# A decoder layer on eight cores: finer dependency records, loads in order of need, seven block products in half of the down projection, norm gains applied at the transposes, and the causal mask as a minimum

## The reference, cut to what matters

```python
n = rms_norm(h, tm_pre_g)                        # sub-layer 1
u, v, q, k, v_att, g_a, g_b = jnp.split(n @ w_in, IN_SPLITS, axis=-1)
u = jax.nn.gelu(u); v = layer_norm(jax.nn.gelu(v), ln_v_g, ln_v_b)
y_a = chunked_spatial_gating(u, v, w_spatial, b_spatial) @ w_branch_a
y_b = moba_attention(partial_rope(q), partial_rope(k), v_att) @ w_branch_b   # causal inside a block
y = (sigmoid(g_a) * y_a + sigmoid(g_b) * y_b) @ w_tm_out
h = h + rms_norm(y, tm_post_g)
...
h = h + rms_norm(cross_attention(rms_norm(h, ca_pre_g), rms_norm(mem, mem_norm_g), ...), ca_post_g)
n = rms_norm(h, ffn_pre_g)
y = (silu(n @ w_gate) * (n @ w_up)) @ w_down     # hidden width 5632
h = h + rms_norm(y, ffn_post_g)
```

## Time and profile before

| | |
|---|---|
| three runs | 3659.61, 4012.02 and 4272.59 us |
| median of the three | 4012.02 us |
| profiled execution, slowest core (core 3) | span 3663.7 us |
| spans of the eight cores | 3637.2 to 3663.7 us |
| mean granted TensorE clock, die 0 and die 1 | 0.983 and 0.984 of full speed |
| PE busy | 3425.0 us, 93% |
| DVE, ACT busy | 46%, 33% |

### The profile page before, as it was taken

How to read it: one execution, slowest core, us unless ns; L and a number is a source line. 1 busy time by engine, 2 the same in 40 slices (tenths; PEclk the granted TensorE clock), 3 DMA queues, 4 the chain that set the end, 5 groups by cost and what they waited for, 6 DMA issues and landing times.

```text
span 3663.7 us, 52891 instructions; the slowest of 8 cores (3637.2 to 3663.7 us)
## 1 busy us (share of the span) xinstructions
PE 3425.0 (93%) x17866; PEld 1641.4 (45%) x17866; DVE 1691.9 (46%) x3470; ACT 1201.3 (33%) x2157; POOL 226.8 (6%) x306
## 2 busy tenths in 40 slices
PE   5989999999888899999887999999999988999997
PEld 3534444444355544545543444444444433444443
DVE  3764465222267746444776555555555620001222
ACT  4633323334477600445652222222222220000110
POOL 1100000000000000000110000000000010000000
PEclk9999999999999999999999999999999999999999
DMA  9225566666742354545665545554454556346564
GB/s 195 74 37 92 96 108 116 110 105 105 136 99 76 82 145 133 152 149 172 172 178 87 94 85 98 87 88 83 83 98 81 93 187 221 105 141 231 210 220 157
DMA packets 339097, 455.97 MB, mean 124 GB/s; under 512 B 29456, under 2 KB 288784, under 8 KB 317712
## 3 DMA queue, kind: packets, MB, share of 16 engines
q0 software_dynamic: 192048, 157.30, 28.4%
q1 hardware_dynamic: 146784, 295.29, 25.0%
HBM read 475.60 MB, written 148.90 MB: 170 GB/s over the span
## 4 chain that ended last, share of the span: by engine, by line
PE 77%; DVE 9%; DMA 6%; issue 4%; ACT 3%; DVEq 0%; POOL 0%; ACTq 0%; SPq 0%; POOLq 0%
PE ps L316 76%; DVE acc L342 2%; DVE fw0r L336 1%; DMA wv<-w_in 1%; PE ps L319 1%; DVE fw2r L336 1%; DMA ht<-HIDT 1%; ACT ffs L329 1%; DMA fw0r<-w_fg 1%; DMA fr0r<-w_fg 1%; DMA HIDT<-ffo 1%; DMA memx<-mem 1%; DVE fpf L332 0%; DVEq L262 0%; DMA gto<-gains 0%
## 5 line engine op out<-in xcount | busy, mean ns | idle before, releaser
L316 PE MATMUL ps<-wd,ht 128*128 128x512 f16 x2816 | 614.4, 381 | 30.5 <-DMA ht<-HIDT 29.7
L316 PEld LDWEIGHTS ps<-wd,ht 128*128 128x128 f16 x2816 | 276.3, 98 | 368.5 <-issue 40.7
L349 ACT COPY fpf<-ps 128x512 f32<-128x512 f32 x336 | 196.1, 584 | 504.6 <-PE ps L316 504.6
L316 PE MATMUL ps<-n1op,ws1r 128*128 128x512 f16 x1024 | 235.7, 383 | 11.0 <-ACT pf L349 11.0
L316 PE MATMUL ps<-n1op,ws0r 128*128 128x512 f16 x1024 | 234.1, 381 | 3.8 <-ACT pf L349 3.8
L349 ACT COPY pf<-ps 128x512 f32<-128x512 f32 x256 | 149.6, 586 | 268.6 <-PE ps L316 267.4
L316 PE MATMUL ps<-RBH,ma 128*128 128x512 f16 x1024 | 226.2, 379 | 0.0
L332 DVE TENSOR_TENSOR fpf<-ps,fpf 128x512 f32<-128x512 f32 x168 | 115.6, 688 | 195.9 <-PE ps L316 158.3
L316 PE MATMUL ps<-n1op,ws0t 128*128 128x512 f16 x768 | 178.1, 382 | 11.0 <-DVE n1op L332 7.5
L329 ACT ACTIVATE junk<-ps 128x512 bf16<-128x512 f32 x128 | 76.1, 595 | 333.8 <-PE ps L316 331.3
L329 ACT ACTIVATE pT<-ps 128x512 bf16<-128x512 f32 (+1 forms) x320 | 160.5, 531 | 69.6 <-PE ps L316 67.1
(11 more groups left out here) (226 smaller groups left out, 4831.1 us busy)
## 6 DMA issues: line engine op xcount, KB each, us to landing
ht<-HIDT SPq DMA_DIRECT2D x40, 1408.0 KB, 7.8
H<-yr SPq DMA_DIRECT2D x32, 1024.0 KB, 9.1
HIDT<-ffo SPq DMA_DIRECT2D x88, 256.0 KB, 8.8
WDH<-w_fd POOLq DMA_DIRECT2D x44, 512.0 KB, 14.3
ws0r<-w_in POOLq DMA_DIRECT2D x16, 1024.0 KB, 13.2
ws1r<-w_in POOLq DMA_DIRECT2D x16, 1024.0 KB, 13.4
GS<-stgh SPq DMA_DIRECT2D x64, 256.0 KB, 4.6
xr<-x SPq DMA_DIRECT2D x16, 1024.0 KB, 6.7
```

Source lines behind the costliest of these rows:

```text
L316: self.S.add("pe", lambda e: e.matmul(out, lhsT, rhs, start=start, stop=stop, **kw), reads, writes)
L349: self.S.add("act", lambda e: e.copy(out, in_), reads, writes)
```

## The change

- **Records.** Tiles that one engine writes in pieces get a record for each piece (`parts=4` for the attention accumulators, `yr`, `cob`, `cqt`), so a piece waits for its own piece. Some DMA semaphores are marked `exact`: a wait is for that DMA and not for the newest on the semaphore. Waits of one instruction on one semaphore are merged.
- **Loads.** x tiles 2 to 5 and the constants wait for parts of `wv`; `wv` comes in eight DMAs; x uses four buffers; the `w_sp` transposes come later. The memory tokens are normed and transposed during blocks 20 to 30 and kept in HBM (`MTD`), their weights are converted to f16 in HBM (`WKH`) during blocks 2 to 17. The first head is loaded ahead of these weights, and `gto` beside `wo`.
- **First blocks.** Two gate blocks come first; the first two products of both quads are done before the third of either. The sum S1 and the slots' sums are in the plan. The same interleaving starts the FFN.
- **Mask.** `dm` is 0 above the diagonal and 3e38 elsewhere; DVE takes the minimum with the exponentials instead of the second matmul.
- **Norm gain of the FFN.** `fgain` is gone; the copy after the transposes multiplies by the gain (`f_c2`).
- **Down projection.** Columns 0 to 1023 go by seven block products, with blocks of 22x128 hidden by 128 tokens and 22x128 hidden by 256 columns. The weights are kept in a layout of their own (`WD7`).
- **End.** The last 512 columns are done in two halves, and the last tile's four output parts have a record and a semaphore each.
- Durations and latencies in the plan are new numbers; the DVE statistics of the layer norm have two instructions fewer.

```diff
-            if so.sem is p.dsem:
+            if so.sem is p.dsem and not so.exact:
...
     blocks = []
+    for i in range(2):
+        blocks.append(("g", i, 5120 + i * 256))
...
+            gate = {2: [bwv[kc][0] for kc in range(8)], 4: [bwv[kc][1] for kc in range(8)], 6: env[("x", 4)][1] if tt == 6 else []}
+            B.dma("sp", ap, x[tt * 128:(tt + 1) * 128, :], d, gate.get(tt, []), bufs)
...
-            if diag:
-                B.mm(ps_[:, 0:128], identb[:], dm[:], False, True, [bcon2], [psb_])
...
+        if diag:
+            def f_cm(pk=pk):
+                p_, pb_ = env[pk]
+                B.tt(p_[:, 0:128], p_[:, 0:128], dm[:], ALU.min, [pb_, bcon3], [pb_])
+            ex = T("dve", 0.1, f_cm, [ex], si - 2, lat=0.2)
...
-                    B.cp(f_.t[:, :, c4 * 128:(c4 + 1) * 128], p[:].bitcast(F16).rearrange("p (k t) -> p k t", k=8), [pb], [f_.b[c4]])
...
+                    g3 = gcols[:, 3, half * 8:half * 8 + 8].unsqueeze(2).to_broadcast([128, 8, 128])
+                    B.tt(f_.t[:, :, c4 * 128:(c4 + 1) * 128], p[:].bitcast(F16).rearrange("p (k t) -> p k t", k=8), g3, ALU.mult,
+                         [pb, bconst], [f_.b[c4]])
...
-    def fgain(sl):
-        for kc in range(KC):
-            w_ = sl.raw[:, kc, :]
-            bb = sl.bq[kc // 8]
-            B.ts(w_, w_, gcols[:, 3, kc:kc + 1], None, ALU.mult, None, bb + [bconst], bb)
...
     def wd_cast(r):
-        B.dma("pool", WDH[r * 128:(r + 1) * 128, :], w_fd[r * 128:(r + 1) * 128, :], dwd[r % 4], [], [bWDH[r]])
+        kh, kk = r // KD2, r % KD2
+        B.dma("pool", WD7[kh, :, :, kk * 256:(kk + 1) * 256].rearrange("c p n -> p c n"),
+              w_fd[r * 128:(r + 1) * 128, 0:1024].rearrange("p (c n) -> p c n", c=4), dw7[r % 4], [], [bWD7[r]])
+        B.dma("pool", WDH[r * 128:(r + 1) * 128, :], w_fd[r * 128:(r + 1) * 128, 1024:2048], dwd[r % 4], [], [bWDH[r]])
...
+        def prod(bank, a, wi, start):
+            a_, w_ = hop(m, a), W[wi]
+            for k in range(KD2):
+                B.mm(bank[0][:, 0:256], a_[:, k * 128:(k + 1) * 128], w_[:, k * 256:(k + 1) * 256], start and k == 0, k == KD2 - 1,
+                     [a_.b, w_.b], [bank[1], mark] if wi == 0 and k == 0 else [bank[1]], skip_group_check=True)
...
+        if m == 7:
+            hook(4, lambda: (wsum(1, "T1"), wsum(1, "T2"), hsum(8, "S1"), hsum(8, "S2")))
+            hook(5, lambda: (wsum(1, "T3"), hsum(8, "S3")))
+            hook(6, lambda: hsum(8, "S4"))
+            hook(7, lambda: wsum(1, "T4"))
+        elif m < 15:
+            hook(4, lambda: [hsum(m + 1, w_) for w_ in ("S1", "S2", "S3")])
+            hook(6, lambda: hsum(m + 1, "S4"))
+        if m < 14:
+            hook(5, lambda: [load_q(m + 2, w_) for w_ in (A11, A21, A12)])
+            hook(7, lambda: load_q(m + 2, A22))
...
+        prod(X, A11, 0, True)
+        s1 = snap(X)
+        prod(Z, A12, 2, True)
+        add(0, 0, Z, s1)
+        prod(X, S2, 5, False)
+        s2 = snap(X)
+        prod(Y, S1, 4, True)
+        s5 = snap(Y)
+        prod(X, A21, 1, False)
...
+            hq, hqd = hb, hd
+            if np_ > 1:
+                hq, hqd = Buf("hrq"), B.dsem("fin%d" % q)
+                hq.last_w = hb.last_w
```

More of the change, by code:

```diff
@@ L680, in _program @@
     YP = Res("yp", [item(yl, i) for i in range(2)])
+    YE = Res("ye", [item(ye, i) for i in range(2)])
     VP = Res("vp", [item(vn, i) for i in range(2)])
@@ L940, in quad @@
         hook(7)
+    def quad(*a_):
+        for _ in quad_steps(*a_):
+            pass
     def h_u(blk, p):
```

782 lines of the change are left out of this document (488 added, 294 removed).

## The result

| | before | changed |
|---|---|---|
| runs | 3659.61, 3693.9, 3711.56, 4012.02, 4265.86, 4272.59 | 3467.76, 3475.8, 3478.21, 3877.55, 4022.22, 4075.51 |
| median | 3861.79 us | 3677.88 us |
| cores of one undisturbed die, profiled execution | 3637.2 to 3663.7 us | 3455.3 to 3467.3 us |

Three of the six runs of each kernel take some 10 to 18% longer than its shortest, and since the changed kernel's three, its profiled run among them, have the cores of one die at a lower granted clock (in the profile 0.86 to 0.87 on cores 4 to 7), only the other three, called undisturbed here, are compared, and the changed kernel's rows are of core 1. The ratio is 0.943 with an interval of 0.930 to 0.957: faster.

A forecast was written before the change was run, and what follows sets the result against it. PE, busy 3425 of 3663.7 us, was taken as the bound. Terms summing to 177 us, less 10 for what the rows don't show, took 167 from 3659.6 and gave 3493 us, range 3440 to 3578.

The forecast's parts named there:

- Products and loads of the down projection: Down projection, columns 0 to 1023: 2464 products of 256 columns at 0.109 us replace 1408 of 512; 31 us net saved.
- the 6 us for new waits: Down projection: allowance of 6 us set against the products' gain, for snapshots, operand sums and loads.
- The weight load rival: Down projection: weight loads show behind 256-column products; all 241 us more (chance 0.02), a quarter 62 us (0.03).
- FFN's end, first half and middle: FFN's end to down projection's middle: earlier token-tile loads 24 us, narrower products 31, middle wait gone 7.
- End: Last output parts: three waits of 2.26 us for the store before go with a record each; 7 us.
- Cross-attention and FFN: Waits from weight-slot gains, `gto` and sums go, with slow clock: cross-attention 26 us, FFN start 14, FFN steady part 11.
- Attention: Attention: 13 us saved, mostly mask products and half the small bubbles; 10 at its start from loading the first head earlier.
- the rival that its step on DVE lies in the open: Attention: the mask's minimum on DVE is waited for, 38 us lost instead of 13 gained; chance 0.08.
- v stage and first blocks: Before the attention: 20 us from v-stage loads and sums, 14 from moving memory-token norming into blocks 20 to 30.
- The term of 20: v stage: products run before the late `w_sp` transposes, and end-of-stage sums and waits mostly go; 20 us saved.
- Waits did not move on: Rival, v stage to FFN's end: new waits appear behind removed ones, half of 121 us comes back, 3553 us; chance 0.18.
- More than forecast: Rival, whole kernel: most terms come near their high ends, 3430 us; chance 0.09.

The follow-up runs named there:

- `b_att_both`: Kernel before with four records per attention accumulator and output tile and the attention planner's new numbers: attention stretch 386.4 us net against 450.4, whole-kernel ratio 0.984.
- `att_records`: Changed kernel with one record in place of four for each attention accumulator and output tile: attention stretch 436.4 us net against 379.1.
- `b_acc_records`: Kernel before with four records in place of one per attention accumulator and output tile: attention stretch 418.6 us net against 450.4, whole-kernel ratio 0.997.

## Why the prediction was right and wrong

- **Products and loads of the down projection.** 0.109 us a product, 38.0 us for seven in place of eight (36.9 forecast), and of the 6 us for new waits only 0.7 came: the sums of DVE lie beside the products (134.7 of 269.9 us busy). The weight load rival is refuted. FFN's end, first half and middle together gave 71 where 62 were forecast: 37 by the products, the waits of 22.88 and 5.70 us whole, and the other 5 or 6 by the clock.
- **End**: 5.8 of 7.
- **Cross-attention and FFN**: mechanism right, size off. Forecast 26 + 14 + 11 = 51, measured 74.5, beyond the sum of the high ends, 70. Net it is 50.6, of which the gains are 36 to 39, finer records 5, the interleaving 5, the planner's numbers 3 to 7. The slow clock of the stretch went almost whole, 23.9 of 25.6 us, where I had counted a part.
- **Attention**: the step that failed most, "mostly the mask products and half of the small bubbles", 13, and 10 at its start, against 73 measured. Two faults. I bounded the gain by PE's idle time, 49.6 us, but a product in a short run counts 219 ns as busy where its columns take 54. In this stretch PE's busy time fell by 32 us beside 41 us of idle time. The length less the products' columns and the slow clock, from the first score product to the last product with `v`, would have given 81.7 us as the room, and 21.0 are left. And I priced the records by the rows in which a releaser stands, 3 us, although the idle time of 28.9 us ahead of 288 accumulations was in front of me. What the runs showed in place of this step: the records and the planner's numbers, neither of which the step names as its main part, make 64 us (`b_att_both`). The mask, which I took for the main part, is worth 1 us net; the rival that its step on DVE lies in the open didn't come either, but `att_records` shows that it would have with one record (20.2 us).
- **v stage and first blocks**: 34 forecast. The profiled core is 27.9 us longer; the six cores with the same loads and without a stretch at 0.81 need 970.0 to 980.0 us, where the kernel before needs 992.4 to 1001.7: 21 us shorter on the mean. "The new order cannot make that earlier" is wrong as a statement on `wv`, whose last part landed 43 and 34 us after its issue in other orders, against 55.7. The term of 20 failed all the same, since the wait moved from `w_sp` to `wv`, 10.6 us in all, 5.22 of it at 50 us, where no wait over 5 us was to be left: the stage takes 177 us on the mean before and after (177 and 171 net), so the term should have been 0 to 6. It also rests on a misread row: PE had done 32 products with `wv` before the last gap, not 40. The blocks took 796 to 802 us in place of 817 to 825, some 20 us for the 14 forecast.
- **The clock**: no term had a slow stretch that the kernel before's profile doesn't show. The two on the profiled core count 61 us of slow clock and cost some 50: cores of the changed kernel without one lie at 3408 to 3415 us, and the profiled core at 3467.3. So the total was near (167 forecast, 181 to 192 measured) by luck: a gain forecast some 80 us too small (3659.6 to 3408 or 3415 is 245 to 252) and a loss of 50 to 60 us that was not foreseen nearly cancel.
- **The number**: the forecast was made for executions like the profiled one, and gave nothing for the others. Among the former 3493 was 15 to 25 us too high, inside the range; the median of all six, 3677.9, is 100 us above the range's end.
- **Rivals.** Waits did not move on in the stretches from the attention to the end; they did at `stg` (4.30 us) and `wv` (10.6 us). "More than forecast" (3430 us) was nearest for the cores without a stretch at 0.81 (3408 to 3415 us); for the time itself, 3467.8 to 3478.2, it was the forecast.

## What to carry to other kernels

Where one engine works on independent pieces of one tile, look at the idle time ahead of the group, even if it has no releaser: a record for each piece gave 29 to 57 us for two changed lines, and an order by a planner pays only once its assumed times fit and the chains are free. Take a stage's room from its length less its columns, not from PE's idle time. Compare stages by length and net of slow clock, on cores with as much slow clock as each other, and compare several executions before a difference in total is put down to work.

## What was not expected of the hardware

- A granted clock of 0.81 for stretches of some 160 us, with PE 98% busy (159.68 of 163 us), on some cores and in some executions, always close behind a wait of PE and a spell at the lower level. A change in the order of DMAs in the first 60 us raised the cores with a mean clock of 0.993 or more from 6 of 48 to 32 and 38 of 48, with the work to the attention's start some 5 us faster at most.
- `b_acc_records` won 31.8 us net in its stretch, yet its undisturbed runs are only 0.3% below those of before (0.994 to 1.000): on the slowest core of its profile the first half of the down projection runs at 0.88 and has 44 us of slow clock, where the kernel before has 15.4.
- Small accumulations on DVE overlap when they don't wait for each other: 286 of 344 ns in 81 us.
